# Second mixer in rounds of seven block products, with other first and last slots

## The reference, cut to what matters

```
layer 0: h += attention/HGRN2 mixer (hn @ ab_w_in ... @ ab_w_out)
layer 1: b, c, g = split(hn @ conv_w_in, 3)        # conv_w_in: 2048 x 6144
         u = c * g
         y = b * conv3(u)                          # centred, width 3, over tokens, per channel
         h += y @ conv_w_out                       # 2048 x 2048
both:    h += square(relu(hn @ mlp_w_up)) @ mlp_w_down     # 2048 x 8192, 8192 x 2048
out = rms_norm(h) * final_norm_g
```

## Time and profile before

| | us |
|---|---|
| median of 3 runs | 2291.95 |
| profiled execution | 2291.84 |
| its span, first to last instruction | 2289.8 |
| TensorE busy | 2256.8 (99%) |
| VectorE busy | 1759.3 (77%) |
| ScalarE busy | 1291.2 (56%) |
| POOL busy | 289.8 (13%) |

### The profile page before, as it was taken

One profiled execution on the slowest core, in us unless ns is written; L12 is line 12 of the kernel. 1 busy time (PEld: TensorE's weight loads), 2 busy tenths in 40 slices (PEclk: granted clock), 3 DMA queues, 4 the chain that ended last, 5 costly groups with the idle time before them and its releaser, 6 DMA issues.

```text
span 2289.8 us, 31124 instructions
## 1 busy us (share of the span) xinstructions
PE 2256.8 (99%) x11429; PEld 1902.5 (83%) x11429; DVE 1759.3 (77%) x1882; ACT 1291.2 (56%) x1655; POOL 289.8 (13%) x409
## 2 busy tenths in 40 slices
PE   8999999999999999999999999999999999999997
PEld 7888888878788888888889999998788888888886
DVE  5778788866888888888875564657888888888885
ACT  5555555537666566566555333435665665665663
POOL 4444555510000000000000000000000000000000
PEclk9999999999999999999999999999999999999999
DMA  9555555556778678678656555556687787787754
GB/s 261 166 158 153 159 153 147 167 168 217 210 239 275 193 238 276 197 232 280 182 167 208 180 176 195 190 183 221 182 279 202 224 285 201 223 278 209 219 172 154
DMA packets 324321, 470.49 MB, mean 205 GB/s; under 512 B 13257, under 2 KB 144626, under 8 KB 318706
## 3 DMA queue, kind: packets, MB, share of 16 engines
q1 hardware_dynamic: 318114, 424.92, 56.8%
q0 software_dynamic: 6048, 44.04, 10.3%
q10 hardware_dynamic: 48, 0.02, 0.0%
HBM read 422.79 MB, written 2.10 MB: 186 GB/s over the span
## 4 chain that ended last, share of the span: by engine, by line
PE 90%; DVE 7%; ACT 1%; issue 1%; SPq 1%; DMA 0%; DVEq 0%; POOL 0%; POOLq 0%; ACTq 0%
PE pair L433 18%; PE pair L437 18%; PE pair L435 17%; PE m L1083 7%; PE m L1088 7%; PE m L1086 7%; PE pair L456 3%; PE pair L460 3%; PE pair L458 3%; DVE raw L1781 2%; DVE w_lo L524 2%; PE m L460 1%; PE m L458 1%; PE m L456 1%; PE m L934 1%
## 5 line engine op out<-in xcount | busy, mean ns | idle before, releaser
L520 ACT ACTIVATE w_hi<-raw 128x1024 fp32r<-128x1024 f32 x648 | 663.3, 1056 | 494.5 <-DVE raw L1781 242.9
L524 DVE TENSOR_TENSOR w_lo<-raw,w_hi 128x1024 fp32r<-128x1024 f32 x648 | 764.2, 1221 | 204.5 <-ACT w_hi L520 202.5
L412 DVE TENSOR_TENSOR w_lo<-raw,w_hi 128x1024 fp32r<-128x1024 f32 x320 | 400.1, 1267 | 273.5 <-ACT w_hi L401 272.2
L401 ACT ACTIVATE w_hi<-raw 128x1024 fp32r<-128x1024 f32 x320 | 337.3, 1060 | 447.1 <-PE pair L437 278.9
L433 PE MATMUL pair<-w_hi,yT_hi 128*128 128x512 f32 x1280 | 506.5, 396 | 2.5 <-DVE h L1544 0.9
L437 PE MATMUL pair<-w_hi,yT_lo 128*128 128x512 f32 x1280 | 499.1, 390 | 0.0
L435 PE MATMUL pair<-w_lo,yT_hi 128*128 128x512 f32 x1280 | 498.5, 389 | 0.0
L433 PEld LDWEIGHTS pair<-w_hi,yT_hi 128*128 128x128 f32 x1280 | 240.4, 188 | 56.1 <-issue 7.2
L437 PEld LDWEIGHTS pair<-w_hi,yT_lo 128*128 128x128 f32 x1280 | 240.3, 188 | 51.1
L435 PEld LDWEIGHTS pair<-w_lo,yT_hi 128*128 128x128 f32 x1280 | 240.7, 188 | 47.5
L433 PE MATMUL pair<-w_hi,xT_hi 128*128 128x512 f32 x640 | 255.9, 400 | 0.0
(11 more groups left out here) (168 smaller groups left out, 3104.7 us busy)
## 6 DMA issues: line engine op xcount, KB each, us to landing
raw<-in_mlp_w_up SPq DMA_DIRECT2D x128, 1024.0 KB, 7.0
raw<-in_mlp_w_down SPq DMA_DIRECT2D x256, 512.0 KB, 6.3
raw<-in_ab_w_in SPq DMA_DIRECT2D x256, 256.0 KB, 4.0
raw<-in_conv_w_in SPq DMA_DIRECT2D x48, 1024.0 KB, 5.1
raw<-raw POOLq DMA_DIRECT2D x42, 1024.0 KB, 8.7
raw<-in_ab_w_out SPq DMA_DIRECT2D x64, 256.0 KB, 4.3
raw<-in_conv_w_out SPq DMA_DIRECT2D x16, 1024.0 KB, 5.1
h<-in_x SPq DMA_DIRECT2D x4, 512.0 KB, 5.9
```

The lines of the kernel that those rows point to most:

```text
L401: nc.scalar.activation(w_hi[:, ring], raw[:, slot, 2 * k:2 * k + 2], ACT.Copy).then_inc(hi_ready, 1)
L412: nc.vector.tensor_tensor(w_lo[:, ring], raw[:, slot, 2 * k:2 * k + 2], w_hi[:, ring].bitcast(F32), ALU.subtract).then_inc(lo_ready, 1)
L520: nc.scalar.activation(w_hi[:, entry % HALVES], src, ACT.Copy).then_inc(hi_ready, 1)
L524: nc.vector.tensor_tensor(w_lo[:, entry % HALVES], src, w_hi[:, entry % HALVES].bitcast(F32), ALU.subtract).then_inc(lo_ready, 1)
```

## The change

- The second mixer becomes a stage like the MLPs (`stage(st)`, st = 0, 1, 2; CONV = 1). c and g of a block of 512 channels are the two halves of columns of a P round, x stationary; their plain form for block 0 fills 8 plain slots, blocks 1 to 3 come in 3 rounds. D slots of odd rounds are b's product for two blocks (4 slots each), those of round 2 and of the last 8 slots the output product for two blocks of y each. So the stage has 8 + 3 x 22 + 8 = 82 slots, of which the 42 of the P products are half as long.
- With x stationary, tokens stand on partitions. u (made by VectorE, `make_u`) and b (copied out by ScalarE, `copy_b`) are turned by four transposes a half block into M[3] (`conv_turn`), in the order TURNS; ScalarE copies u out (`copy_u`), VectorE multiplies b in from M[3] (`times_b`). A turn waits until the one before it is read. POOL's multiplication and rstd2's row go.
- x's unscaled copies lie in `raw` where block B22 of round 1 goes for st = 1 and 2, so that B22's load waits for `x_low`; the loads of D0 and D1 stand behind it in SP's queue.
- P5's second half sum leaves SUMS_DVE and becomes a POOL DMA, in all three stages.
- First slot: its first entry is multiplied before the second block's transposes, and its load has a semaphore of its own for the first half; the parameter loads come two slots later.
- Last two D slots: `last_down` does token tile 0 of both slots before token tile 1. The final gain is multiplied in ahead (`times_gain`), rstd is made per token tile, VectorE and ScalarE scale two of the four pieces each, and both SP and ScalarE store.

The core of the diff (turns, stage programs, and the end):

```diff
+CONV = 1
+CONV_ROUNDS = CB
+STAGE_ROUNDS = [ROUNDS, CONV_ROUNDS, ROUNDS]
+OUT_PRODUCT = [(0, 0), (1, 0), (0, 1), (1, 1), (2, 0), (2, 1), (3, 0), (3, 1)]
-SUMS_DVE = [("P5", 0), ("P5", 1), ("P7", 0), ("P6", 0), ("P4", 0)]
+SUMS_DVE = [("P5", 0), ("P7", 0), ("P6", 0), ("P4", 0)]
...
+        TURNS = [("u", 0, 1), ("u", 0, 0)]
+        for n in (0, 2):
+            TURNS += [("b", n, 0), ("b", n, 1), ("u", n + 1, 1), ("u", n + 1, 0), ("b", n + 1, 0),
+                      ("b", n + 1, 1), ("u", n + 2, 1), ("u", n + 2, 0)]
...
 load_block (SP):
                         if free is not None:
                             sp.wait_ge(lo_ready, 2 * (free + k) + 2)
+                        elif block == "B22":
+                            sp.wait_ge(s_low, 4 * st + 2 * k + 2)
...
 POOL:
-                    for name in ("P7", "P6", "P4"):
+                    for name in ("P5", "P7", "P6", "P4"):
...
                         if name == "P7":
-                            pool.wait_ge(sums.sem, sums.at("P51", nth(layer, r)))
+                            pool.wait_ge(added["P5"], 16 * (nth(st, r) + 1))
...
 PE:
+                def conv_turn(which, n, tt):
+                    k = turned(which, n, tt)
+                    if k == 1:
+                        pe.wait_ge(c_lo, made(0, ROUNDS - 1, "C11"))
+                    elif TURNS[k - 2][0] == "u":
+                        pe.wait_ge(cv_uT, u_made(*TURNS[k - 2][1:]))
+                    else:
+                        pe.wait_ge(cv_y, b_made(*TURNS[k - 2][1:]))
+                    if which == "u":
+                        pe.wait_ge(cv_u, u_made(n, tt))
+                    else:
+                        pe.wait_ge(cv_b, b_made(n, tt))
...
+                def out_product(r, m):
+                    if m in (0, 2):
+                        pe.wait_ge(cv_lo, r - 1 + half)
...
+                    for r in range(1, last):
+                        for name in ROUND:
+                            if name[0] == "P":
+                                product(r, name)
+                            elif r % 2:
+                                b_product(r, int(name[1]))
+                            else:
+                                out_product(r, int(name[1]))
+                            if r == 1 and name == "P1":
+                                conv_turn("u", 0, 0)
+                            if r % 2 and name in ("P3", "D4"):
+                                conv_turn("b", r - 1, int(name == "D4"))
+                            if r == 2 and name in ("P1", "D0"):
+                                conv_turn("b", 1, int(name == "D0"))
+                            if name in ("P2", "D6"):
+                                conv_turn("u", r, int(name == "P2"))
...
 ACT:
+                            if r == 1 and name == "D0":
+                                copy_u(0, 0)
+                            if r % 2 and name == "D6":
+                                y_hi(r - 1)
+                            if r == 2 and name == "D1":
+                                y_hi(1)
+                            if name in ("D6", "D7"):
+                                copy_u(r, int(name == "D6"))
+                            if name == "D4":
+                                copy(r, "C21")
+                            split(slot + 2)
+                            if r == 1 and name == "P1":
+                                copy_u(0, 1)
+                            if name[0] == "P":
+                                split(slot + 3)
...
+                            if r % 2 and name in ("P3", "D4"):
+                                copy_b(r - 1, int(name == "D4"))
+                            if r % 2 and name == "D7":
+                                copy_b(r, 0)
+                                copy_b(r, 1)
...
 DVE:
+                            if name == "D7":
+                                tap(r, 0)
+                                tap(r, 1)
+                                split(slot + 2, (0,))
+                                if r != 2:
+                                    tap(r, 2)
+                                split(slot + 2, (1,))
+                            else:
+                                split(slot + 2)
+                            if name[0] == "P":
+                                nxt = {"P1": "P5", "P5": "P7", "P7": "P6", "P3": "P4"}.get(name)
+                                if nxt:
+                                    block_sum(r, nxt)
+                                split(slot + 3)
+                            if r == 1 and name in ("D0", "P5", "D1"):
+                                tap(0, ("D0", "P5", "D1").index(name))
+                            if r == 3 and name == "P1":
+                                tap(2, 2)
+                            if r == 2 and name in ("D0", "P5"):
+                                times_b(1, int(name == "P5"))
+                            if r == 2 and name == "P7":
+                                y_lo(1)
...
+                            if name in ("P4", "P2"):
+                                make_u(r, int(name == "P4"))
+                            if r % 2 and name in ("D4", "D5"):
+                                times_b(r - 1, int(name == "D5"))
+                            if r % 2 and name == "D6":
+                                y_lo(r - 1)
...
 PE, start and end:
-                gain_transpose_pe(0, 1)
...
+                    if (c, j) == (0, 0):
+                        head_product(c, j, 0, 0, 0, 0, (0,))
+                        gain_transpose_pe(0, 1)
+                        head_product(c, j, 0, 0, 0, 0, (1,))
+                        continue
...
+                def last_down():
+                    for tt in range(NT):
+                        for n in range(4):
+                            m, k = 6 + n // 2, n % 2
...
+                            if tt == 0 and n == 3:
+                                mm.then_inc(fin_product, 1)
```

More of the change, by code:

```diff
@@ L662, in _ @@
[L662 to L670 removed]
+                    load_down(last, m)
@@ L671, in _ @@
+            for st in range(3):
+                stage(st)
+            for tt in range(NT):
+                for half in range(2):
+                    sp.wait_ge(fin_dve, 2 * tt + half + 1)
+                    store(sp, tt, half)
             sp.wait_ge(stored, 16 * CB * NT)
@@ new lines, in b_product @@
+                def b_product(r, m):
+                    half = m // 4
+                    if m % 4 == 0 and r > 1:
+                        pe.wait_ge(pair_read[half], before + 2)
+                    elif m == 0:
+                        pe.wait_ge(cv_c, 1)
+                    elif m == 4:
+                        pe.wait_ge(cv_u, u_made(0, 0))
+                    multiply(pe, slot_of(st, r, f"D{m}"), 0, 0, x_at, xT_hi, xT_lo, 4 * (m % 4),
+                             pair[half], m % 4 == 0, m % 4 == 3)
@@ new lines, in out_product @@
+                def out_product(r, m):
+                    cb, half = OUT_PRODUCT[m]
+                    if m < 2:
+                        pe.wait_ge(cv_b, b_made(r - 2 + cb, 1))
+                    elif half == 0:
+                        pe.wait_ge(pair_read[cb % 2], before + r - 1)
+                    if m in (0, 2):
+                        pe.wait_ge(cv_lo, r - 1 + half)
+                    for k in range(2):
+                        multiply(pe, slot_of(st, r, f"D{m}"), 0, 0, y_at, yT_hi, yT_lo, 4 * half,
+                                 pair[cb % 2], half == 0 and k == 0, half == 1 and k == 1, (k,))
+                        if r == last and m == 0:
+                            conv_turn("b", 3, k)
@@ new lines, in _ @@
+            for st in range(3):
+                stage(st)
+            for tt in range(NT):
+                if tt == 0:
+                    dve.wait_ge(fin_product, 1)
+                else:
+                    wait_product(dve, TOTAL - 1, 0, 0)
+                cb = CB - 1
+                nc.vector.scalar_tensor_tensor(
+                    out=h[:, tt, cb * 512:], in0=pair[cb % 2][:, tt], scalar=rstd2[:, 3, tt:tt + 1],
+                    in1=h[:, tt, cb * 512:], op0=ALU.mult, op1=ALU.add).then_inc(fin_added, 1)
+                dve.wait_ge(fin_added, tt + 1)
+                times_gain(cb, tt)
+                mean = meansq[:, tt:tt + 1]
+                dve.wait_ge(sq_done, (4 * CB + CB - 1) * NT + tt + 1)
+                nc.vector.tensor_reduce(mean, sumsq[:, tt], AX_X, ALU.add).then_inc(fin_rstd, 1)
+                dve.wait_ge(fin_gain, 2 * (CB - 1) + tt + 1)
+                dve.wait_ge(fin_rstd, 3 * tt + 3)
+                for half in range(2):
+                    nc.vector.tensor_scalar(hg[:, tt, half], hg[:, tt, half], rstd[:, 4, tt:tt + 1],
+                                            None, ALU.mult).then_inc(fin_dve, 1)
```

846 lines of the change are left out of this document (422 added, 424 removed).

## The result

The changed kernel takes 2328.68 us (median of four runs, 2327.06 to 2330.26); the kernel before, on the same chip, 2291.98. The ratio is 1.0161, with a 95% interval of [1.0149, 1.0173]. It is slower, by 37 us. The forecast was 2296 with a range up to 2312. It leaned to slower, with a chance of 0.41; the size was far too small. The profiled execution is one of 2327.06 us with a span of 2325.3, and it stands 35.5 us of span over that of before.

The account below looks back on a forecast made before the run. TensorE's issue slots and the waits ahead of them bound the kernel (busy 2256.8 of 2289.8 us). Against 2291.84: mixer +15, P5 -11.4, MLP 2 +3.2, first slot 0, last slot -4.9, clock +2, sum +4: 2296 us, range 2266 to 2312.

Parts of the forecast that it names:

- The waits of order: Second mixer: TensorE waits following from instruction order alone (2 x 4.7, 2 x 3.35, 3.4, 3.95), 23.5 us.
- Rival 1: Mixer's turns wait less than read: 2261 us, or 2278 with half of the waits; chance 0.25.
- The mixer's size without the clock: Second mixer: 343 us without waits plus 39 of waits, 382 in all, 15 longer than before; bounds 366 to 388.
- The clock: TensorE's half rate after six long waits of 3.4 to 7.6 us: 0 to 6 falls, 0 to 8.4 us, taken as 2.
- rival 3: TensorE's clock falls in every long wait: 2302 us; chance 0.12; sign, a granted clock under 1 in the mixer.
- P5's accumulate: MLP rounds: P5's second sum as POOL DMA lands mostly in time, 0.95 us a round saved over 12 rounds, -11.4.
- rival 2: P5's accumulate lands late, deciding from 8.4 us after issue: 2307 to 2319 us; chance 0.12; sign, MLP rounds at 85 or more.
- Rival 4: Relieving VectorE of P5's sum does nothing, waits return further on, 0.2 us a round left: 2305 us; chance 0.11.
- MLP 2's first round: D0's load queued behind B22 comes late and delays TensorE's turn: +3.2 us (2 to 4.5).
- The ends: First slot 0 us (between -1.2 and +0.3); last slot, the tail after the final add, -4.9 us (3.5 to 6).

Follow-up runs that it names:

- turns_later: The changed kernel with b's turns one unit later on TensorE, each behind the product that follows: 2302.73 us, 1.0044 of the kernel before.
- ylo_earlier: The changed kernel with VectorE's y_lo(1) moved from unit P7 of round 2 to unit D1: 2319.60 us, 1.0127 of the kernel before.
- loads_first: The changed kernel with D0's and D1's loads ahead of B22's in SP's queue for mixer and MLP 2: 2318.78 us, 1.0116 of before.
- all_four: The changed kernel with the edits of p5_back, turns_later, loads_first and ylo_earlier together: 2272.60 us, 0.9917 of the kernel before.
- p5_back: The changed kernel with P5's second half sum back on VectorE: 2319.86 us, 1.0123 of the kernel before.
- pe_waits: The kernel before with one artificial TensorE wait, of varied length, ahead of P2 in ten MLP rounds: 2422.76 us, ratio 1.0570.
- p5_pool_hold: The kernel before with P5's second half sum as a POOL accumulate DMA and D2's loads held until it lands: 2296.03 us, ratio 1.0018.
- p5_pool_alone: The kernel before with one edit, P5's second half sum as a POOL accumulate DMA: 2291.41 us, ratio 0.9996.
- all_four_pool_hold: all_four, but P5's second sum stays a POOL DMA and D2's loads wait for its landing: 2283.72 us, 0.9965 of the kernel before.

## Why the prediction was wrong, step by step

**The waits of order: right.** The turn behind P3 comes 10.17 us after P3 starts (10.15 forecast), in rounds 1 and 3 (1521.82 to 1531.98); D4's turn waits from 1341.99 to 1345.22 (3.2; forecast 3.35); D2 of round 2 starts 14.28 us after P7, 8.85 over its own 5.44 (forecast 7.6 and 1.5); the turn behind D0 has 5.5 us, more than the 3.9. D0 of round 1 is 3.0 late (forecast 3.8). P7 to D2 in round 1 is 7.33, two of the taps' microseconds. turns_later, ylo_earlier and loads_first each take one or more of these away, and the time, or with ylo_earlier most of it, goes with them: shown, not only argued. Rival 1, that the other engines catch up, is refuted.

**The mixer's size without the clock: right.** In all_four the same matmuls and turns of the mixer keep TensorE busy for 347.14 us, at full clock; in the kernel after for 358.88. So 11.7 us of the 393.85 are half clock, and 382.1 is what is left; the forecast was 382. That it fits to a tenth is luck: the waits over 0.3 us, from start to start, add up to 37.0 where the sum had 39, and in all_four 8.1 us of such waits leave 345.6 for the rest, where it had 343.

**The clock: mis-sized.** "0 to 6 falls cost 0 to 8.4. I take 2." There were seven stretches in the mixer, 11.7 us or 1.7 each, and one in MLP 2. Every wait of 3.2 to 7.6 us brought it; I valued what no row of before could show at a sixth of its price. The traces show it for this kernel, with waits counted from one matmul's start to the next: the record has 38 of 3.45 to 17.88 us within full work (seven in the kernel after, seven in p5_back, six each in loads_first and ylo_earlier, two in turns_later, ten in pe_waits), and 38 times half clock; those up to 2.1 us never brought it; of those between, some did (2.22 and 2.92 in loads_first, 3.22 in the kernel after), some did not (2.48 and 3.23 in turns_later). The Trainium skill's "TensorE: Matmul & The Clock Gate", Part 1, says that the array drops to half rate when it has been idle and recovers under load. The traces agree: 0.43 against 0.23 us from matmul to matmul. This is rival 3, and its sign, a granted clock under 1 in the mixer, came.

**P5's accumulate: this step failed.** "Lands 6.9 to 9.4 later: mostly in time", -11.4. Measured, MLP 1 is 2.3 longer and MLP 2's rounds behind the first 4.9 (10.6 less the first round's 5.7): +7.2, 18.6 off, the largest error of the sum. The gain at D0 to P5 came (0.48 a round), and in rounds that land in time the round is 84.00, the 84.0 forecast. But P5's transfer took 8.2 to 10.4 us in the rounds behind the first, and the limit is 8.4. I had the limit right in rival 2 (the sum itself had 933.35, some 8.2 us after the issue) and took the spread of three other transfers as if its lower half were this one's. Their median alone, 8.7, lay beyond the limit: the row already said that more than half would be late. The spread has a pattern that the row does not tell: P7's accumulates of before land after 6.9 to 7.3 us in MLP 1, where no packet of the "instruction" queue lies beside one, and after 8.3 to 8.5 in MLP 2, where each has one. So this is rival 2, with its sign, rounds of 85 and more in which ScalarE's split waits for the accumulate. Rival 4, that the relief does nothing, is refuted by the round of 84.00. By the Trainium skill, "DMA: Bandwidth & Descriptors", Anatomy of one DMA, a transfer of 1 MB issued by GpSimd would take an estimated 4.4 us (2.0 and 1 MB at 436 GB/s); no accumulate here took under 6.9, so that figure would have misled further.

**MLP 2's first round: right in kind.** TensorE of the kernel after, as against the earlier trace rows:

```profile
1672.08 0.39 PE L1139 MATMUL m<-w_hi,xT_lo 128*128 128x512 f32 x1
1678.18 1.09 PE L1192 MATMUL m<-ident,blk 128*128 128x128 f32 x4 [5.70 <-issue]
```

From start to start this is 6.09 us against 2.10 before, so +4.0, within the 2 to 4.5 given. With the half clock behind it P5 starts 7.24 us after D0 where it was 5.56, and the round is 5.7 longer in all. The view names no releaser ("issue"); that loads_first takes the wait back to 2.03 shows that it was D0's late load.

**The ends: right.** MLP 1 starts 0.9 later with 0 forecast, and in the other seven kernels with the same first slot it starts at 533.4 to 534.3, with 534.25 before, so that even the 0.9 is this execution's; the tail is 4.8 shorter with 4.9 forecast. VectorE behind the last matmul of the kernel after, as against the earlier trace rows: one token tile is added where two were, and two scalings are left where eight were, with two more on ScalarE.

```profile
2317.22 0.75 DVE L2147 SCALAR_TENSOR_TENSOR h<-pair,rstd,h 128x512 f32<-128x512 f32 x1 [1.75 <-PE pair L1175]
...
2320.00 0.88 DVE L2159 TENSOR_SCALAR raw<-raw,rstd 128x512 f32<-128x512 f32 x2 [1.03 <-POOL rstd L889]
```

**The form of the range: wrong.** Rivals 2 and 3 were priced one by one, 2307 to 2319 and 2302, and the upper end of 2312 reached to one of them. They are not alternatives: late landings and half clock came together: 2296 + 18.6 (P5) + 9.7 (clock in the mixer) + 2.5 (MLP 2's first round) + 0.9 (the start) is 2327.7, and the profiled execution took 2327.06. When two rivals on one side exclude each other in nothing, the range must hold their sum.

**What stays open.** Two things lengthen the accumulate: loads beside it (6.9 to 7.6 us without, 8.1 to 8.8 with them), which p5_pool_hold shows by an edit, and packets of the "instruction" queue, which the traces only show beside it. A run that moves these packets is missing. So is the reason why they fall into P5's transfer in all twelve rounds of the two MLP stages but one in the kernel after, and in none of MLP 2's in p5_pool_alone, and how far they make the scatter between executions.

## What to carry to other kernels

When work is moved to a transfer, compare its deadline with the median landing of its like and not with the shortest: here a limit of 8.4 against a median of 8.7 us turned a forecast gain of 11 into a loss of 7. And look at the scatter of the executions as well as at their median: it grew from 1 us to 8 in p5_pool_alone, where the round came to hang on a transfer. When instructions of one engine are set by hand into an order, put each consumer one unit behind the point at which a trace of the queue says its input is ready; the four places mended here were one line or a few each and worth 56 us. Count a long wait of TensorE with the half clock behind it, which here came with each of the 38 waits of 3.45 us and more and cost some 2 us a time, and look at the stages one by one, since a change that gains 4 us in one and loses 4 in another looks like nothing.

## What the runs showed of the hardware

- The half clock mostly begins while TensorE waits (at 739.0 in the wait from 735.0 to 740.5), and in some cases just behind the wait (0.4 us in the kernel after, 0.8 at the most in loads_first). Once work is back, 3.0 to 6.1 us of it run slow in pe_waits by the record of the clock, whatever the length of the wait was.
- An accumulating DMA of 1 MB within SBUF landed in 6.9 us at the least and 13.9 at the most (p5_pool_hold), with a median of 8.7 before and in the kernel after, though its issue occupies POOL for 0.86 us only.
- Held loads cost the others: the second and third such DMA of a round take 11.1 and 13.4 us when four weight loads of 512 KB are issued beside them.
- Where a 16 KB packet of the "instruction" queue lies beside such a DMA, it lands later: 8.5 to 9.3 us with one and 6.9 to 7.6 without, where no load runs beside it (p5_pool_hold and all_four_pool_hold, 15 and 9 cases). 15 of its 16 semaphore updates come as early as without the packet; the last is the late one.
